# Moving a memory projection into the expert loop, and transposing h before its final norm

## The reference, cut to what matters

```python
# end of the first block
x = x + hierarchical_moe(rms_norm(x, norm_ffn[l]), ...)      # 32 experts, top 2 of a group of 8
h = rms_norm(x, norm_final)
# start of the second block
h = h + 0.5 * swiglu(rms_norm_2(h, ffn1_norm_g[0]), ffn1_w_gate[0], ffn1_w_up[0], ffn1_w_down[0])
# later, in each of two layers
k, v = split(rms_norm_2(mem_2, mem_norm_g[layer]) @ w_mem_kv[layer], 2)
k = rms_norm_2(k.reshape(B, M, 4, 64), k_g)
```

## Time and profile before

| | |
|---|---|
| three runs | 1711.61, 1712.66, 1713.93 us (median 1712.66) |
| profiled execution | 1711.31 us, span of its instructions 1709.5 us |
| busy in the span | PE 1586.1 us (93%), DVE 939.8 (55%), ACT 690.7 (40%) |
| DMA | 413 MB, mean 242 GB/s |
| chain that ended last | PE 68%, DMA 21%, DVE 5%, ACT 4% of the span |

### The profile page before, as it was taken

One profiled execution on the slowest core, in us unless ns is written; L12 is line 12 of the kernel. 1 busy time (PEld: TensorE's weight loads), 2 busy tenths in 40 slices (PEclk: granted clock), 3 DMA queues, 4 the chain that ended last, 5 costly groups with the idle time before them and its releaser, 6 DMA issues.

```text
span 1709.5 us, 30570 instructions
## 1 busy us (share of the span) xinstructions
PE 1586.1 (93%) x12545; PEld 1279.1 (75%) x12545; DVE 939.8 (55%) x1612; ACT 690.7 (40%) x1038; POOL 32.7 (2%) x42
## 2 busy tenths in 40 slices
PE   6999999787888887999999999999999999899999
PEld 5988876554555555788888678888788889678887
DVE  4887451011111111477667867676766677667766
ACT  5556451011001100444545465445545463754543
POOL 3000000000000000000000200000000000000000
PEclk9999999999999999999999999999999999999999
DMA  9744379999999999856464625564464653236460
GB/s 296 239 155 165 129 305 427 429 428 429 429 429 429 427 429 426 310 185 209 161 218 156 173 99 182 186 203 166 148 217 162 210 173 126 73 123 213 159 217 25
DMA packets 166637, 413.00 MB, mean 242 GB/s; under 512 B 5879, under 2 KB 131148, under 8 KB 154284
## 3 DMA queue, kind: packets, MB, share of 16 engines
q1 hardware_dynamic: 164512, 407.99, 64.0%
q0 software_dynamic: 1824, 4.03, 0.8%
q10 hardware_dynamic: 236, 0.06, 0.0%
HBM read 410.27 MB, written 1.78 MB: 241 GB/s over the span
## 4 chain that ended last, share of the span: by engine, by line
PE 68%; DMA 21%; DVE 5%; ACT 4%; issue 1%; SPq 0%; DVEq 0%; ACTq 0%
DMA odd_expert<-in_w_up_dram 19%; PE bank L1290 18%; PE bank L650 10%; PE bank L651 10%; PE bank L652 10%; PE bank L1294 9%; PE bank L1043 3%; DMA odd_expert<-in_w_gate_dram 2%; PE bank L1068 1%; ACT whi L1509 1%; DVE wlo L1979 1%; DVE x L2017 1%; PE bank L664 1%; PE bank L833 1%; PE bank L1057 1%
## 5 line engine op out<-in xcount | busy, mean ns | idle before, releaser
L1290 PE MATMUL bank<-x,whi 128*128 128x512 f32 x1408 | 356.4, 393 | 1.2 <-DVE x L2017 0.9
L1290 PEld LDWEIGHTS bank<-x,whi 128*128 128x128 f32 x1408 | 255.8, 189 | 50.9 <-issue 2.0
L2520 DVE TENSOR_TENSOR wlo<-raw,whi 128x2048 fp32r<-128x2048 f32 x120 | 271.4, 2289 | 32.6 <-ACT whi L1827 27.2
L1827 ACT ACTIVATE whi<-raw 128x2048 fp32r<-128x2048 f32 x120 | 225.4, 1913 | 57.9 <-PE bank L652 57.9
L1294 PEld LDWEIGHTS bank<-x,wlo 128*128 128x128 f32 x1408 | 193.7, 190 | 13.5
L1294 PE MATMUL bank<-x,wlo 128*128 128x256 f32 x1408 | 200.8, 282 | 0.0
L1979 DVE TENSOR_TENSOR wlo<-raw,whi 128x2048 fp32r<-128x2048 f32 x67 | 154.3, 2312 | 62.8 <-ACT whi L1509 62.2
L1509 ACT ACTIVATE whi<-raw 128x2048 fp32r<-128x2048 f32 x67 | 127.0, 1908 | 35.0 <-PE bank L652 29.3
L650 PE MATMUL bank<-whi,hh_hi 128*128 128x512 f32 x352 | 138.1, 392 | 3.1 <-DVE hh_lo L2505 3.1
L651 PE MATMUL bank<-whi,hh_lo 128*128 128x512 f32 x352 | 137.5, 391 | 0.0
L652 PE MATMUL bank<-wlo,hh_hi 128*128 128x512 f32 x352 | 137.0, 389 | 0.0
(11 more groups left out here) (351 smaller groups left out, 2302.9 us busy)
## 6 DMA issues: line engine op xcount, KB each, us to landing
raw<-in_ffn_w_gate_dram SPq DMA_DIRECT2D x44, 1024.0 KB, 5.4
raw<-in_ffn_w_up_dram SPq DMA_DIRECT2D x44, 1024.0 KB, 6.6
raw<-in_ffn_w_down_dram SPq DMA_DIRECT2D x44, 1024.0 KB, 6.2
raw<-in_w_gate_dram SPq DMA_DIRECT2D x16, 2048.0 KB, 20.9
raw<-in_w_up_dram SPq DMA_DIRECT2D x16, 2048.0 KB, 24.2
raw<-in_w_down_dram SPq DMA_DIRECT2D x16, 2048.0 KB, 24.4
odd_expert<-in_w_gate_dram SPq DMA_DIRECT2D x16, 2048.0 KB, 26.5
odd_expert<-in_w_up_dram SPq DMA_DIRECT2D x16, 2048.0 KB, 26.4
```

The lines of the kernel that those rows point to most:

```text
L1290: pe.matmul(bank[:, :], hi[:, k, :], x_both[x][:, k, :, :].rearrange("p b n -> p (b n)"), start=k == 0, stop=False, skip_group_check=True)
L1827: act.activation(whi[:, c0_ % SPLIT, :], raw[:, c0_ % RAW, :], ACT.Copy).then_inc(hi_ready, 1)
L2520: dve.tensor_tensor(wlo[:, c0_ % SPLIT, :], raw[:, c0_ % RAW, :], whi[:, c0_ % SPLIT, :].bitcast(F32), ALU.subtract).then_inc(lo_ready, 1)
```

## The change: what it does

1. The layer-0 keys and values are made like those of layer 1: 16 pieces in all, two a group, after the second and after the third expert's `down`. Layer 1 takes the first four groups, layer 0 the last four. The 2 MB of layer-0 weights are loaded into the same tile `mem2_w` in the middle of the experts (ahead of expert 17's weights), and no longer at their end.
2. The norms of the memory's keys (`mem2_key_norms`) are made ahead of the last expert's hidden tile, and no longer beside the FFN's first matmuls.
3. `h` is transposed as it stands after the adds, without its final row scale; the evacuation multiplies by a new column gain `G_JOIN`, the product of both norms' gains. The final norm's scale is applied to `h` later, and the FFN's row scale becomes the product of both.
4. All six first FFN chunks are issued behind the last expert, and on VectorE the split of chunk 0 stands ahead of the adds, that of chunk 1 behind them.

```diff
-G_END = G_TAP + CONV_TAPS + LATE_TAPS * (CONV_TILES - 1)
+G_JOIN = G_TAP + CONV_TAPS + LATE_TAPS * (CONV_TILES - 1)
+G_END = G_JOIN + KT
...
-        PIECE = 2 * CW // (EXPERTS // EG)
+        PIECES, FIRST_GROUPS = 2 * EXPERTS // EG, EXPERTS // EG // 2
+        PIECE = 2 * CW // (PIECES // 2)
... (SyncE)
-            with sp.Fori(1, EXPERTS // 2) as y:
+            load_mem2(1)
+            middle = EXPERTS // 4
+            with sp.Fori(1, middle) as y:
                 load_experts(y, 0)
                 load_experts(y, 1)
+            load_experts(middle, 0)
+            sp.wait_ge(m2_piece, PIECES // 2)
+            load_mem2(0)
+            load_experts(middle, 1)
+            with sp.Fori(middle + 1, EXPERTS // 2) as y:
...
             sp.wait_ge(main["y_full"], 2 * EXPERTS - 2)
-            for half, slot in enumerate(MEM2_SLOT):
-                src = ins["w_mem_kv_2"][0].rearrange("(k p) n -> p k n", p=P)[:, :, CW * half:CW * half + CW]
-                sp.dma_start(raw[:, slot, :].rearrange("p (k n) -> p k n", k=KT), src).then_inc(in_m2w[half], 16)
-            for c in range(moe_at, moe_at + 4):
+            for c in range(moe_at, moe_at + RAW):
                 load_chunk(c)
... (GpSimd)
+            r1 = G_JOIN - G_DW - P
+            pool.dma_start(rows_c[r1:r1 + KT, :], ins["norm_final"].rearrange("(k p) -> k p", p=P)).then_inc(in_sgu, 16)
... (TensorE)
-                    if e == 1:
-                        mem2_piece(g)
+                    if e in (1, 2):
+                        mem2_piece(layer, g, e - 1)
...
-            mem2_rows(0, ps[6])
-            mem2_rows(1, ps[7], (0,))
-            turn(h, ((h_tile, 1), (h_ready, 3)))
-            mem2_rows(1, ps[7], (1,))
+            keep_busy(4, ps[6])
+            turn(h, ((h_added, 1), (h_added, 2)))
... (ScalarE)
+                    if last and e == EG - 1:
+                        act.wait_ge(m2_ms, 1)
+                        act.activation(krt, kms, ACT.Sqrt).then_inc(m2_root, 1)
                     expert_silu(main, 4 * g + e + 1)
...
-            round_to(moe_at + 1)
+            round_to(moe_at + 2)
             act.wait_ge(moe_done, 1)
-            row_stats(h, ((h_added, 1), (h_added, 2)))
-            round_to(moe_at + 2)
+            unscaled_stats(((h_added, 1), (h_added, 2)), 1, G_JOIN)
...
-            unscaled_stats(((h_tile, 1), (h_ready, 3)), 1, G_FFN1)
-            mem2_out()
-            act.wait_ge(m2_ms, 1)
-            act.activation(krt, kms, ACT.Sqrt).then_inc(m2_root, 1)
+            row_stats(h, ((h_tile, 1), (h_ready, 3)))
             swiglu(0, mem2_keys)
... (VectorE)
+            split_to(moe_at + 1)
             dve.wait_ge(moe_done, 1)
...
-            split_to(moe_at + 1)
-            dve.wait_ge(h_added, 2)
+            split_to(moe_at + 2)
+            split_turned(1, G_JOIN)
             row_scale()
+            link(dve.tensor_copy(final_rstd, rstd))
             dve.wait_ge(in_late, 64)
             for tt in range(TT):
                 ins_ = dve.scalar_tensor_tensor(h[:, tt, :], h[:, tt, :], rstd[:, tt:tt + 1], gain_b, ALU.mult, ALU.mult)
                 ins_.then_inc(h_tile if tt == 0 else h_ready, 1)
             dve.wait_ge(h_ready, 3)
+            row_scale()
+            link(dve.tensor_tensor(rstd, rstd, final_rstd, ALU.mult))
+            diagonal_scales()
```

More of the change, by code:

```diff
@@ L311, in build @@
         outer_half = sem("outer_half")
[L312 removed]
         in_m2r, m2_piece = sem("in_m2r"), sem("m2_piece")
[L314 to L315 removed]
+        m2_turned, m2_x, m2_evac, m2_ms, m2_root, m2_rows, m2_back, m2_k = [sem(n) for n in (
+            "m2_turned", "m2_x", "m2_evac", "m2_ms", "m2_root", "m2_rows", "m2_back", "m2_k")]
         ffn_half, h_tile = sem("ffn_half"), sem("h_tile")
@@ L668, in turn @@
                     pe.wait_ge(*half_ready[0])
-                ahead = min(fills, 4 if first // 4 in WIDE_TURNS + (JOIN_TURN, KV_TURN) else 2)
+                ahead = min(fills, 4 if first // 4 in WIDE_TURNS + (KV_TURN,) else 2)
                 if first // 4 != KV_TURN:
@@ L969, in _, with mem2_piece @@
             linear_outer(26, 3, 3, 0)
[L971 to L985, removed]
+            def mem2_piece(layer, g, i):
+                pe.wait_ge(in_m2r, 16 if layer else 32)
+                pe.wait_ge(m2_evac, 2 * g + (i + 1))
+                at_ = g * (2 * PIECE) + (PIECE * i - (0 if layer else 2 * CW))
                 for tt in range(TT):
                     for k in range(KT):
-                        mm = pe.matmul(ps[5][:, PIECE * tt:PIECE * tt + PIECE], mem2_x[1][:, k, tt * P:tt * P + P],
-                                       mem2_w[:, k, bass.ds(g * PIECE, PIECE)], start=k == 0, stop=k == KT - 1,
+                        mm = pe.matmul(ps[5][:, PIECE * tt:PIECE * tt + PIECE], mem2_x[layer][:, k, tt * P:tt * P + P],
+                                       mem2_w[:, k, bass.ds(at_, PIECE)], start=k == 0, stop=k == KT - 1,
                                        skip_group_check=True)
@@ L1088, in _, with expert_group @@
                 pe.matmul(ps[b][:, :], zeros[:, 0:P], zeros[:, :], start=True, stop=False, skip_group_check=True)
-            def expert_group(g, last, experts=range(EG)):
+            def expert_group(g, last, experts=range(EG), layer=0):
                 for e in experts:
@@ L1124, in expert_group @@
                     gather(1, main, EG * SLOTS, ps[6], sel).then_inc(main["fill"], 1)
-            with pe.Fori(0, EXPERTS // EG - 1) as g:
+            with pe.Fori(0, FIRST_GROUPS) as g:
+                expert_group(g, False, layer=1)
+            with pe.Fori(FIRST_GROUPS, EXPERTS // EG - 1) as g:
                 expert_group(g, False)
@@ L1735, in _, with copy_piece @@
             act.activation(warmth[:, 31:32], ones[:, 0:1], ACT.Copy).then_inc(m2_evac, 1)
[L1737 to L1744, removed]
+            def copy_piece(layer, g, i):
+                act.wait_ge(m2_piece, 2 * g + (i + 1))
+                at_ = g * (2 * PIECE) + (PIECE * i - (0 if layer else 2 * CW))
+                act.activation((kv0, kv1)[layer][:, :, bass.ds(at_, PIECE)],
                                ps[5][:, 0:2 * PIECE].rearrange("p (t n) -> p t n", t=2), ACT.Copy).then_inc(m2_evac, 1)
@@ L1766, in expert_group @@
                     expert_out(main, 8 * g + 2 * e + 1)
-                    if e == 1:
-                        copy_piece(g)
-            with act.Fori(0, EXPERTS // EG - 1) as g:
+                    if e in (1, 2):
+                        copy_piece(layer, g, e - 1)
+            with act.Fori(0, FIRST_GROUPS) as g:
+                expert_group(g, layer=1)
+            with act.Fori(FIRST_GROUPS, EXPERTS // EG - 1) as g:
                 expert_group(g)
-            expert_group(EXPERTS // EG - 1)
+            expert_group(EXPERTS // EG - 1, last=True)
             act.wait_ge(extra_ready, 1)
@@ L2414, in _, with mem2_key_norms @@
             copy_gathered(1, 2)
+            def mem2_key_norms():
+                dve.wait_ge(m2_evac, PIECES + 1)
+                for layer in range(2):
+                    squares = prob[:, layer, :]
+                    link(dve.tensor_tensor(squares.rearrange("p (t n) -> p t n", t=2), k2_t[layer], k2_t[layer], ALU.mult))
+                    ins_ = dve.tensor_reduce(kss[:, 8 * layer:8 * layer + 8], squares.rearrange("p (g d) -> p g d", d=64),
+                                             AX, ALU.add)
+                link(ins_)
+                dve.tensor_scalar(kms, kss, 1.0 / 64, RMS_EPS, ALU.mult, ALU.add).then_inc(m2_ms, 1)
+                dve.wait_ge(m2_root, 1)
+                link(dve.reciprocal(krs, krt))
+                for layer in range(2):
+                    for t in range(TT):
+                        rows_ = k2_t[layer][:, t, :].rearrange("p (g d) -> p g d", d=64)
+                        scale = krs[:, 8 * layer + 4 * t:8 * layer + 4 * t + 4].unsqueeze(2).broadcast_to([P, 4, 64])
+                        ins_ = dve.tensor_tensor(rows_, rows_, scale, ALU.mult)
+                    ins_.then_inc(m2_rows, 1)
             def expert_group(g, last):
@@ L2430, in expert_group @@
                 for e in range(EG):
+                    if last and e == EG - 1:
+                        mem2_key_norms()
                     hidden(main, 4 * g + e + 1)
```

60 lines of the change are left out of this document (21 added, 39 removed).

## The result

The changed kernel takes 1723.16 us (median of 1721.44 to 1724.77), the kernel before 1712.13 us on the same chip (1710.85 to 1713.93): ratio 1.0062, 95% interval 1.0050 to 1.0074. The forecast was 1712.1, no difference. Its profiled execution took 1724.77 us with a span of 1723.0, of which some 2.7 us were lost ahead of 60 us, in matmuls at the start that ran at half clock (0.63 us each from 17.4 to 22.3 us, against 0.39).

The account below looks back on a forecast made before the run. Transfers bound the experts' stage, then a chain, then TensorE from the first `down`. Of 14.1 us removed, 5.4 return as transfers (0.5 regained), 1.5 in VectorE's order, the rest in row-scale chains: 0.6 gained, 1712.1 us, range 1708.6 to 1714.5.

Parts of the forecast that it names:

- The clock: Last expert's gate: the new piece fills 3.8 of 4.36 idle us, so full clock, 1.95 for 3.50 us; 0.5 us gain counted.
- The pieces: Experts' stage: eight more pieces of 3.79 us each lie in TensorE's waits for transfers and cost nothing.
- The load: Experts' weight stream: the 2.10 MB of layer-0 weights make every later landing 5.4 us later.
- The first rival: Experts' stage: the load is hidden and its 5.4 us do not count, giving 1706.7 us; chance 0.13.
- The cover for SyncE's wait: SyncE's load waits about one piece, 3.79 us; some 23 us of transfers queued ahead cover this.
- The keys' norms: VectorE ahead of the last expert's hidden tile: 4.95 us of norms cost nothing, with 3 us of cover.
- The adds: VectorE behind the last expert: start at 708.5 behind chunk 0's split, 1.5 us later than they could.
- the first FFN matmul: TensorE after the adds: starts at 714.1 on the first quarter of transposed h, where before it was 717.39.
- the row scale: Junction: a 5.9 us chain ready at 722.4; TensorE waits 2.5 us, its four matmuls at 722.5 instead of 723.19.
- the first `down`: FFN on TensorE: starts at 730.5 behind VectorE's hidden tile, 0.9 us earlier than 731.38.
- The second rival: Junction: chunk 0 lands no sooner behind the last weights, adds start 4.6 us later, 1716.7 us; chance 0.06.
- The third: TensorE's row-scale wait: half clock after it adds up to 1.55 us, 0.7 over the hidden tile, 1712.8 us; chance 0.10.

## Why the prediction was wrong

**The clock** is the step that failed: the piece was to fill 3.8 of the 4.36 us ahead of the last gate, so that the gate would run at full clock. It failed through the reading of one row. I took the 4.36 us for a wait for transfers, which a piece could fill, since the row named a DMA. It was code and landing ending together (the code packet at 683.87, after which other gates start some 1.5 us later, the landing at 684.93, the gate at 685.32): without the branch the gate still waited 2.54 us for its weights, and without the piece the idle in the changed kernel was 4.53. In place of 0.5 gained, the last expert lost four things against the kernel without a branch: the idle at the branch 4.31, the idle in the gate 2.53, the gate at half clock 1.9 (3.20 + 0.63 against 1.95) and the spread 1.7 (5.40 against 3.70). That is 10.4; the closing matmuls came 12.6 us later (719.59 against 707.00), of which 2.2 stood already at the piece (690.43 against 688.25), most of it from the start. By the times it is 11 us (1723.16 against 1712.1).

**The pieces** cost nothing where TensorE would wait for weights, as I said. The last one, ahead of the branch, has no such wait: moving it away gave 3.4 us. And the program had become longer, which my sum had no term for: it moved the code against the 16 KB blocks, and a break that the kernel before doesn't show fell into the last gate.

**The load** was 5.6 against 5.4. Another 0.5 us is spread over the rest of the stage (176.8 against 176.3), but the kernel without the load has it too. The first rival (it is hidden) falls: without it the last `down` came 5.6 us sooner. The cover for SyncE's wait was right, though the issue was held for 15 us and not for a piece.

**The keys' norms** stayed hidden: without the branch the last expert's silu still waited 2.62 us for TensorE behind the second table load. **The adds, the first FFN matmul, the row scale, the first `down`** came within 0.5 us of their numbers, in the kernel without a branch on the clock (adds at 708.29 against 708.5), in the kernel after counted from the adds. The second rival (chunk 0 no sooner) did not come about. The third did in the kernel after, and was cheap: behind the wait of 2.14 us the gate of the second tile ran at half clock (3.07 us against 2.09 without a branch, where a wait of 2.13 was not followed by half clock). The junction took 22.15 us in place of 21.75, 0.4 more, where the rival had 0.7; without a branch TensorE had waited 0.80 us for VectorE's hidden tile, and this slack took up part of it.

So without the branch the change is worth about what was forecast, 1.4 us by the medians (1713.53 to 1712.1), or 2.9 when the branch is left out of both kernels (1715.04 to 1712.1); and none of the kernels that keep the overflow rounds beats the kernel before by more than can be measured (1.0000 at best).

## What to carry to other kernels

A branch on an engine can lead to code that the engine doesn't hold: look for the packets of the instruction queue at every idle behind one, and don't count such an idle as room, whatever releaser the row names. Put the branch where the engine waits for something that ends later, with long instructions queued ahead of it, and check it again after any change in code length. When a stage is bound by transfers, price a moved load by its own packets; here it was given back in full although it was issued some 250 us ahead of the stage's end.

## What the runs showed of the hardware that was not expected

TensorE gets its code in blocks of 16,384 bytes, which the profile lists among the packets of the core's 16 DMA engines. A branch to code that isn't held took 5.9 to 6.4 us in each of the ten profiles that have one. Some 3.4 to 3.9 us passed before the packet began, 1.1 us were the packet, and the branch ended 1.4 us behind it. What stood idle was 2.7 to 4.9 us, by how much work was queued ahead of the branch. The DMA engines were busy around each of these packets (share 0.99 to 1.07), so what such a branch costs beside idle transfer queues no run shows.

Code that runs on in a straight line is fetched ahead: the kernel without a branch has such packets at 684.60 and 695.62 and no idle beside them. A second idle came only where the jump landed near a block's end, 25 to 52 matmuls ahead of it.

The Trainium skill, "Advanced Engine Details and Errata" (ISA Cache, in the section on the sequencer), gives lines of 16 KB, which hold 256 instructions, and says that there are two of them. The packets agree with the size. The number does not agree: one round of the experts' loop in the kernel before is 1,391 recorded instructions of TensorE, over five such lines, and it ran six times from 290 to 643 us without a code packet. The same page (Control Flow Timing) gives 51 ns for a branch that is always taken and 108 for one that compares. The loop's branches took 76 to 233 ns; the branch to the last expert's code, which was not there, took over fifty times the 108.
